# Prompt attention on VectorE: taking a unit's scores out of PSUM ahead of an older unit's scan chain

## What is computed

```python
z = jnp.einsum('bqhd,bkhd->bhqk', q, kc) * (HEAD_DIM ** -0.5) + bias
log_beta = jnp.where(valid, jax.nn.log_sigmoid(z), -jnp.inf)
log_keep = jnp.where(valid, jax.nn.log_sigmoid(-z), 0.0)
later = lax.cumsum(log_keep, axis=3, reverse=True) - log_keep
a = jnp.exp(log_beta + later)
out = jnp.einsum('bhqk,bkhd->bqhd', a, vc)
```

## Time and profile before

| what | value |
|---|---|
| median of 3 timed runs | 2414.48 us |
| range of the runs | 2412.24 to 2419.23 us |
| time of the profiled execution | 2420.88 us |
| its span, first to last instruction | 2419.2 us |
| PE busy | 2279.2 us, 94% of the span |
| DVE busy | 1199.8 us, 50% |
| ACT busy | 924.3 us, 38% |
| DMA queue q1, hardware | 234.08 MB, 34.2% of 16 engines |

### The profile page before, as it was taken

One profiled execution on the slowest core, in us unless ns is written; L12 is line 12 of the kernel. 1 busy time (PEld: TensorE's weight loads), 2 busy tenths in 40 slices (PEclk: granted clock), 3 DMA queues, 4 the chain that ended last, 5 costly groups with the idle time before them and its releaser, 6 DMA issues. The chain is left out here.

```text
span 2419.2 us, 44912 instructions
## 1 busy us (share of the span) xinstructions
PE 2279.2 (94%) x17646; PEld 2065.4 (85%) x17646; DVE 1199.8 (50%) x2114; ACT 924.3 (38%) x1637; POOL 147.1 (6%) x197
## 2 busy tenths in 40 slices
PE   7999999999888799999999999999998888999997
PEld 7999999777556599999999999988775557999997
DVE  6433265336665555342453333753466654743425
ACT  5223252324435554222452233432243455632333
POOL 0000010002222000000000000100112200000000
PEclk8999999999989899999999999999898999999999
DMA  5323334226866543232333233431467746332333
GB/s 134 82 69 92 100 98 151 71 88 189 251 188 181 173 126 82 69 97 78 105 76 101 69 87 93 124 120 53 132 207 231 239 132 196 88 88 69 87 104 93
DMA packets 384957, 290.97 MB, mean 120 GB/s; under 512 B 51808, under 2 KB 368392, under 8 KB 384272
## 3 DMA queue, kind: packets, MB, share of 16 engines
q1 hardware_dynamic: 368128, 234.08, 34.2%
q0 software_dynamic: 16128, 54.54, 7.2%
q10 hardware_dynamic: 528, 0.02, 0.0%
HBM read 274.99 MB, written 13.58 MB: 119 GB/s over the span
## 5 line engine op out<-in xcount | busy, mean ns | idle before, releaser
L222 PE MATMUL ps<-h_hi,w_hi 128*128 128x288 f32 x2400 | 716.7, 299 | 16.4 <-PEq L177 10.4
L223 PE MATMUL ps<-h_lo,w_hi 128*128 128x288 f32 x2400 | 708.2, 295 | 0.0
L224 PE MATMUL ps<-h_hi,w_lo 128*128 128x288 f32 x2400 | 708.1, 295 | 0.0
L222 PEld LDWEIGHTS ps<-h_hi,w_hi 128*128 128x128 f32 x2400 | 450.4, 188 | 23.7 <-issue 16.9
L246 DVE TENSOR_TENSOR w_lo<-w_raw,w_hi 128x2048 fp32r<-128x2048 f32 x143 | 327.8, 2292 | 262.0 <-ACT w_hi L240 261.6
L223 PEld LDWEIGHTS ps<-h_lo,w_hi 128*128 128x128 f32 x2400 | 450.6, 188 | 1.0
L224 PEld LDWEIGHTS ps<-h_hi,w_lo 128*128 128x128 f32 x2400 | 450.3, 188 | 0.0
L240 ACT ACTIVATE w_hi<-w_raw 128x2048 fp32r<-128x2048 f32 x143 | 272.9, 1908 | 125.9 <-PE ps L224 77.5
L222 PE MATMUL ps<-f_a_hi,w_hi 128*128 128x288 f32 x1024 | 302.7, 296 | 0.0
L224 PE MATMUL ps<-f_a_hi,w_lo 128*128 128x288 f32 x1024 | 301.6, 295 | 0.0
L223 PE MATMUL ps<-f_a_lo,w_hi 128*128 128x288 f32 x1024 | 301.5, 294 | 0.0
(11 more groups left out here) (365 smaller groups left out, 3226.1 us busy)
## 6 DMA issues: line engine op xcount, KB each, us to landing
w_raw<-in_w_ffn_in SPq DMA_DIRECT2D x132, 512.0 KB, 5.2
w_raw<-in_w_ffn_out SPq DMA_DIRECT2D x80, 512.0 KB, 4.9
sa_vn<-in_cache_sb_v SPq DMA_DIRECT2D x256, 128.0 KB
w_raw<-in_w_in SPq DMA_DIRECT2D x52, 512.0 KB, 4.5
sa_vn<-in_cache_win_v SPq DMA_DIRECT2D x96, 128.0 KB
w_raw<-in_w_out SPq DMA_DIRECT2D x24, 512.0 KB, 7.6
sa_kn_early<-in_cache_win_k POOLq DMA_DIRECT2D x72, 128.0 KB
sa_vn<-in_cache_win_v SPq DMA_DIRECT2D x16, 512.0 KB
```

The lines of the kernel that those rows point to most:

```text
L222: pe.matmul(out, stat_hi, mov_hi, start=start, stop=False, skip_group_check=True)
L223: pe.matmul(out, stat_hi, mov_lo, start=False, stop=False, skip_group_check=True)
L224: return pe.matmul(out, stat_lo, mov_hi, start=False, stop=stop, skip_group_check=True)
```

## The change

In `vector_program` of prompt attention the block that issues the scan chain of unit t-2 is moved behind the block that takes the scores of unit t. No instruction, wait or buffer is added, removed or altered; the order on DVE changes in each tick in which both blocks issue something, which are the odd ticks t = 3, 5, ... 31, fifteen in each of the two layers. The queues of PE, ACT, POOL and SP stay as they are.

```diff
         for t in range(G["ticks"]):
-            u = t - 2
-            if 0 <= u < len(units) and units[u][2] == "stick":
-                s, w = nth[u], width(u)
-                zu, fu = z[:, u % PZ, 0:w], f[:, s % PF, 0:w]
-                dve.wait_ge(S["ln_done"], s + 1)
-                dve.scalar_tensor_tensor(fu, zu, 0.0, fu, ALU.max, ALU.add).then_inc(S["f_done"], 1)
-                dve.wait_ge(S["f_done"], s + 1)
-                dve.tensor_tensor_scan(fu[:, ::-1], one[:, 0:1].to_broadcast([P, w]), fu[:, ::-1], 0.0,
-                                       ALU.mult, ALU.add).then_inc(S["sum_done"], 1)
-                dve.wait_ge(S["sum_done"], s + 1)
-                dve.tensor_tensor(zu, zu, fu, ALU.subtract).then_inc(S["scanned"], 1)
             if t < len(units):
                 i, h, kind = units[t]
...
                     dve.scalar_tensor_tensor(zt[:, w - P:w], score_bank(t)[:, w - P:w], bias[:, h:h + 1], strict[:],
                                              ALU.add, ALU.add).then_inc(S["z_ready"], 1)
+            u = t - 2
+            if 0 <= u < len(units) and units[u][2] == "stick":
+                s, w = nth[u], width(u)
+                zu, fu = z[:, u % PZ, 0:w], f[:, s % PF, 0:w]
+                dve.wait_ge(S["ln_done"], s + 1)
+                dve.scalar_tensor_tensor(fu, zu, 0.0, fu, ALU.max, ALU.add).then_inc(S["f_done"], 1)
+                dve.wait_ge(S["f_done"], s + 1)
+                dve.tensor_tensor_scan(fu[:, ::-1], one[:, 0:1].to_broadcast([P, w]), fu[:, ::-1], 0.0,
+                                       ALU.mult, ALU.add).then_inc(S["sum_done"], 1)
+                dve.wait_ge(S["sum_done"], s + 1)
+                dve.tensor_tensor(zu, zu, fu, ALU.subtract).then_inc(S["scanned"], 1)
             for u in G["out_at"].get(t, ()):
```

## The result

| what | before | after |
|---|---|---|
| median of the timed runs, side by side | 2416.86 us (4 runs) | 2450.35 us (4 runs, 2443.00 to 2462.13) |
| ratio | | 1.0156, interval 1.0110 to 1.0202 |
| the same comparison on another chip | 2421.10 us (11 runs) | 2458.35 us (4 runs) |
| its ratio | | 1.0153, interval 1.0135 to 1.0172 |
| span of the profiled execution | 2419.2 us | 2460.5 us |

The changed kernel is slower by 1.5%, some 37 us. Losses and gains in us are in this text a ratio times 2420 us; a difference of two medians can lie some us away from that (in the first comparison it is 33.5 us, the ratio gives 38, in the second both give 37). Its profiled execution is the longest of its four runs (2462.13 us), about 12 us above the median; that has to be kept in mind where its stretches are measured.

The account below looks back on a forecast made before the run. It took waits between engines in a ring, ending with DVE's scan chain, to bound the prompt attention stretches. Per layer 9.6 + 6.8 - 1.3 = 15.1 us, 30 for both, took the median from 2414.48 to 2445 us, range 2424 to 2466.

Parts of the forecast that it names:

- the three worked ticks: Ticks 19, 23 and 31 of prompt attention, followed signal by signal; prices 1.3, 1.1 and 2.3 us.
- What bounds it: PE limits the whole (94% busy); in the two prompt attention stretches no engine is full, waits in a ring bind.
- The three edges: First-stretch waits: ACT's exponential for DVE's chain 27.7 us, PE for DVE's take 3.6, PE for ACT's copy L2360 4.6.
- Tick 19: Chain starts 1.29 us later, moving ACT's exponential and copy L2360, for which PE's L2289 waits: price 1.3 us.
- Tick 23: Chain 2.40 us later; side work hides L2268's delay, but late key copy L2753 holds PE's L2640: price 1.1 us.
- Tick 31: Chain 5.3 us later, behind the take; PE's transposes L2268 move from 824.81 to 827.1: price 2.3 us.
- The sum: Per layer: eight middle-width ticks 9.6 us, four of width 512 6.8, less 1.3 absorbed: 15.1 us; both layers 30.
- rival C: Added PE pauses bring half rate more often, five more drops per layer, about 3 us each: 2475 us; chance 6%.
- sign of being wrong: Stretches keep their length although the chain starts later, or their clock falls clearly below 0.96.
- The absorbed 1.3 us: Late in each stretch PE waits 1.7 us for DMAs; the longest, 1.3 us, absorbs one tick's price.
- the zero for the narrow ticks: Three width-128 ticks priced at zero, as a following 1.9 us PE wait for a DMA swallows their loss.
- The other signs: Expected in the profile after: chain wait toward 50 us, prompt takes, copy waits and stretches up about 15 us, other stages same.

Follow-up runs that it names:

- the delay ahead of the chain: Kernel before plus one reduction over 512 columns, result unused, on DVE ahead of each scan chain: 2432.70 us, ratio 1.0046.
- the same delay ahead of the take: Kernel before plus one reduction over 512 columns, result unused, on DVE between scan chain and take: 2425.03 us, ratio 1.0008.
- the early ticks: Kernel before with the change in ticks 3 to 15 alone (widths 128 and 256): 2435.97 us, ratio 1.0066.
- the late ones: Kernel before with the change in ticks 17 to 31 alone: 2446.38 us, ratio 1.0114.
- only the wait: Kernel before, scan chain also waiting for PE's scores of unit t, take still behind it: 2445.85 us, ratio 1.0110.
- the copy first: Changed kernel with ACT's copy L2360 issued ahead of its exponential L2354: 2438.96 us, ratio 1.0085 of the kernel before.

## Why the prediction was right, and where its sizes were off

The forecast was 2445 us in 2424 to 2466, and the median is 2450. The verdict and its mechanism hold, and the three worked ticks came out to within 0.15 us. The sum lacked a term for the clock, which it had put at nothing, and it priced the ring somewhat too high; that the total came so near is in part luck, since the two go opposite ways.

**What bounds it.** Right. The three edges read from the earlier trace rows behave as named: the delay ahead of the chain costs 11 us, the same delay ahead of the take 2. That PE is busy for 94% of the whole program had no bearing on these stretches.

**Tick 19.** Predicted 1.3 us. The timeline of the changed kernel, to be read against the earlier trace rows:

```profile
768.30 0.91 PE L2260 MATMUL ps<-TR 128*128 128x384 f32 x2
...
773.03 0.69 PE L2289 MATMUL ps<-ident,pa_left 128*128 128x128 f32 x2 [3.10 <-ACT pa_left L2360]
```

```profile
769.25 0.48 DVE L2312 TENSOR_SCALAR pa_z<-ps,pa_left 128x256 f32<-128x256 f32 x1 [0.55 <-PE ps L2260]
...
769.91 0.55 DVE L2320 SCALAR_TENSOR_TENSOR pa_left<-pa_z,pa_left 128x384 f32<-128x384 f32 x1
...
772.07 0.52 ACT L2354 ACTIVATE pa_z<-pa_z 128x384 f32<-128x384 f32 x1 [4.51 <-DVE pa_z L2325]
```

From the scores to L2289 it is 4.73 us (768.30 to 773.03), before it was 3.45 (764.54 to 767.99): 1.28 more. The take starts 0.04 behind the scores' end, the chain 0.66 behind the take, as worked out.

**Tick 23.** Predicted: L2268 covered by side work, and 1.1 us at the key transposes. Against the earlier trace rows:

```profile
789.31 0.91 PE L2260 MATMUL ps<-TR 128*128 128x384 f32 x2
...
794.03 0.55 PE L2268 MATMUL ps<-ident,pa_z 128*128 128x128 f32 x3
...
796.13 1.06 PE L2640 MATMUL ps<-ident,sa_kn_last 128*128 128x128 f32 x8 [0.94 <-ACT sa_kt L2753]
```

Scores to L2268 4.72 us, before 4.64: covered. Scores to L2640 6.82 us, before 5.59: 1.23 more, with ACT's L2753 as the releaser that was named.

**Tick 31.** Predicted 2.3 us. Against the earlier trace rows:

```profile
836.44 1.12 PE L2260 MATMUL ps<-TR 128*128 128x512 f32 x2
...
842.26 0.66 PE L2268 MATMUL ps<-ident,pa_z 128*128 128x128 f32 x4 [2.00 <-ACT pa_left L2360]
```

```profile
837.60 0.62 DVE L2312 TENSOR_SCALAR pa_z<-ps,pa_left 128x384 f32<-128x384 f32 x1 [4.41 <-PE ps L2260]
```

5.82 us from scores to transposes, before 3.55: 2.27 more. DVE stood idle for 4.41 us ahead of the take, with a chain behind it that could have run.

**The sum.** Here a term was missing. It had 15.1 us per layer; the profiled stretch of the first layer is 23.3 longer. The lag of PE's scores (start of L2260 in the tick, counted from the start of the stretch, after less before) against the same sum made up to that tick:

| scores of tick | lag measured | by the prediction's terms |
|---|---|---|
| 11 | 1.2 | 1.2 |
| 12 | 2.9 | 2.4 |
| 15 | 7.8 | 3.6 |
| 23 | 13.3 | 8.4 |
| 31 | 20.9 | 13.4 |
| end of the stretch | 23.3 | 15.1 |

Some 4 us of the 8 that are missing arise between the scores of ticks 12 and 15, and 3 more between 23 and 31. The first place shows what was missing. PE's timeline in the changed kernel:

```profile
730.02 1.04 PE L2640 MATMUL ps<-ident,sa_kn_early 128*128 128x128 f32 x8
...
736.24 0.44 PE L2289 MATMUL ps<-ident,pa_left 128*128 128x128 f32 x2 [2.55 <-ACT pa_left L2360]
...
738.62 0.69 PE L2289 MATMUL ps<-ident,pa_left 128*128 128x128 f32 x2 [0.62 <-ACT pa_left L2360]
739.10 1.92 PE L2640 MATMUL ps<-ident,sa_kn_early 128*128 128x128 f32 x8
```

and the views by engine of the stretch behind it, after, and of 12 us in the same place before:

```profile
739.00:752.00 13.00, 11.55 (x99) 9.02 (x98) 4.54 (x14) 4.63 (x13) 2.44 (x5) 0.52 0.13 42
```

```profile
740.00:752.00 12.00, 8.59 (x112) 7.01 (x112) 6.81 (x21) 6.27 (x19) 4.02 (x8) 1.00 0.45 136
```

After two idle times, of 2.55 and 0.62 us, the eight transposes L2640 take 1.92 us where they took 1.04 nine us earlier. Then PE is busy for 11.55 of 13 us at a granted clock of 0.52, which is its level of 1.2 GHz, and does fewer matmuls than it did before in 12 us at 1.00, its level of 2.4 GHz. From the scores of tick 12 to those of tick 15 it takes 15.2 us (736.51 to 751.74), before 10.4 (739.34 to 749.72). Between 802.7 and 828.0 the granted clock of the changed kernel is 0.66.

So rival C, which had 6%, came in part and beside the forecast, not in its place. The prediction's row for it was one of a whole 3.71 us idle, and it said that such pauses were rarely met; here a shorter one was enough, and a period at half rate could be longer than the about 3 us that C counted. A long pause came as well. In tick 27 the late copy makes PE idle for 3.64 us, where no wait for it was over 1.8 in before, and behind it PE is at half rate again:

```profile
814.24 0.69 PE L2289 MATMUL ps<-ident,pa_left 128*128 128x128 f32 x2 [3.64 <-ACT pa_left L2360]
```

The Trainium skill, page "TensorE: Matmul & The Clock Gate", section "Why this matters for your kernels", has the rule that long gaps between bursts bring the halved clock back. The pause of 3.64 us agrees with it; behind the shorter ones of 2.55 and 0.62 us the clock was halved as well, which that rule alone would not have told.

The prediction had named this as a sign of being wrong: the clock in the stretches falling clearly below 0.96. It fell to 0.85 and 0.86. By its own sign the forecast was therefore incomplete, though its number lay in the range.

How much of the 37 us is the clock can only be estimated. In the profile the idle time of PE grew by 11.4 us per layer, its busy time by 11.9, some of which lies where PE would have waited anyway. And the profiled execution is above the median: the medians have 37 us for both layers, 18 to 19 per layer, the profile 23. The timed runs give a second view. In the second comparison the mean granted clock is 0.9627 for the changed kernel and 0.9705 for before, 0.0078 less. Among runs of one kernel a clock lower by 0.001 goes with about 1.5 us (before) to 1.9 us (changed, eight runs), so by this estimate 12 to 15 of the 37 us go with the clock and 22 to 25 remain. Worked out in the same way (0.9653 and 0.9655 against 0.9708), the early ticks keep 6 to 8 of their 16 us and the late ones 18 to 20 of their 28. That is 24 to 28 together, near the 22 to 25 of the whole, so the clock may be why the two halves seemed to cost too much. Of the 11 us of the delay ahead of the chain 4 to 6 go with the clock too (0.9672 against 0.9701). No experiment holds the clock still while the chain moves, so the split is not shown by a run. The mean granted clock is lower in all kernels with ratios over 1.006: 0.965 to 0.966 with only the wait, only the early and only the late ticks, 0.968 with the copy first.

Against the remaining 22 to 25 us, and 23 us more idle time of PE in the profile, the sum's 30 us for the ring are too many.

**The absorbed 1.3 us.** The DMA waits did vanish (1.9 and 1.7 us in the earlier trace rows, 0.2 in the rows above), and the lag dips to -0.2 at the scores of tick 9; but by tick 11 it is back at 1.2. The sum gave them 1.3 us besides the zero for the narrow ticks; by the wait rows 3.4 us went, so this term was too small rather than too large. What the sum left out beside it is the gain at the take: PE's wait there fell by 2.7 us per layer, and the forecast counted none of it.

**The other signs.** ACT's wait for the chain was to go toward 50 us: 54.9. The take was to start within 0.1 us of the scores' end in every odd tick: in the first stretch it does in all sixteen, by 0.03 to 0.10 us. Both stretches were to be longer by about 15 us: they are by 23.3 and 23.6, and this sign missed by the slower matmuls. PE's waits for ACT's copies were to grow by about 15 us per layer. To the 4.6 us for L2289 these three belong in before:

```profile
PE ps L2689 <- ACT sa_kt L2753: 1.3, 1, 1.3
PE ps L2268 <- ACT pa_left L2360: 1.1, 1, 1.1
...
PE ps L2640 <- ACT sa_kt L2753: 0.6, 1, 0.6
```

That is 7.6 us, and 9.9 + 8.5 + 3.1 + 1.8 = 23.3 after: 15.7 more. So the lateness of the copies was priced at the right size. PE's whole idle time grew by less, 11.4 us, since its waits for the take (2.7 us less) and for the DMAs (3.4 less) went away; what the sum lacked on the other side is the slower work. Stages outside the two stretches were to be the same, and they are to 0.2 us but for the start of the program.

## What to carry to other kernels

Where several in-order engines pass work round in a ring, look up which signal is waited for last in the stretch in question, and keep everything that isn't needed for it behind it in its queue; a move that frees a resource sooner (here the PSUM bank, 3.6 us of waits per layer) can cost more than it gives if it puts a wait ahead of the signal that ends last (27.7 us of waits). Price such a move by the edge's wait rows and two or three ticks followed, then add the slower matmuls that new pauses of TensorE bring: in the profiled run PE's busy time grew by as much as its idle time. If a chain ends last, look for a tick in which it could run earlier: that gained 0.5% here, where the change lost 1.5%.

## What the runs showed of the hardware

Half rate did not need one long pause. It followed idle times of 2.55 and 0.62 us with about 1.8 us of work between them, and it lasted for some 13 us in which PE was busy for 89% of the time. Elsewhere in the changed kernel it followed a single pause of 3.64 us. In before there is a half-rate row behind an idle time of 3.71 us and a full-rate one behind 1.26 us. The mean granted clock of a run and its time go together even for one kernel: in the 69 runs of before beside the experiments, on four chips, a clock lower by 0.001 came with about 1.5 us more (1.3 to 1.8 by chip).
